# Second attention of a two-block kernel: a score bank for each head, query rotations by transfers and GpSimd, scores ahead of the last chunks, more selection rounds beside the queries

## The chip, the core and the metric

The kernel runs on one core of a Trainium2 chip, in one launch. The metric is the device time in microseconds (us); the engines are PE (TensorE), DVE (VectorE), ACT (ScalarE), POOL (GpSimd) and SP (the queue that issues transfers).

## What is computed

The reference chains a recurrent/attention block and a second block of two layers, all in fp32 on 512 positions with a model width of 1024. The change lies in the attention of the second block's first layer. Cut to that:

```
proj = h @ w_in                       # q: 16 heads of 64, k, v: 4 heads, an indexer: qi 8 heads, ki 1, wi 8
q = rope(rmsnorm(q)); k = rope(rmsnorm(k)); qi = rope(qi); ki = rope(layernorm(ki))
# rope: out = x * cos + swap_halves(x) * signed_sin, on all 64 rows of a head
for each block of 128 positions:
    score = sum over 8 heads of relu(qi . ki) * wi         # causal
    sel = the topk = 128 best keys of each position
    logits = q . k / 8, only the selected keys             # 16 heads
    o = softmax(logits) @ v
y = o @ w_out
```

After it come the residual, a gated feed-forward layer, a convolution layer and a second feed-forward layer; most of the time goes into their matrix products.

## The kernel before

**Tiles of weights.** All large products read one stream of weight tiles of 128 x 1024, `Tile(n)`, numbered from 0 to `T_END`. For each tile SP loads `RAW` (`raw`), ACT writes the rounded half `W_hi` (`split_hi`), DVE the rest `W_lo = RAW - W_hi` (`split_lo`, two instructions), and PE runs `linear`: for each of 8 chunks three products into one bank. PE waits on the semaphore `lo_done`, so a late `W_lo` stops it. Each engine has its own program, written out in order, and waits on semaphores.

**Tiles T_QKV2 to T_QKV2 + 16** make the indexer's inputs, keys, values, and last the eight query chunks (tiles T_QKV2 + 9 to + 16; "queries 6 to 13" in the rotation's count, two heads each). Between the products of these tiles PE also does the small work in `in_q(c)`: index scores for the last block of positions (the first four chunks), sums of squares (`query_columns`) and the rotation's product (`rot2`, a 128 x 128 permutation against the chunk, in bank 3).

**The query chunk's path.** ACT takes the bank out (`head_out`: a square, and `QN`); POOL multiplies `QN` by the cosine (`times_cosine`, into `QR`); PE turns `QN` (`rot2`); DVE multiplies the bank by the sine and adds (`turned`, `rope2_out`, into `Q`). POOL also sums the last block's index scores (`index_sum`, a multiply and an add for each head) and takes powers for the norms (`power`).

**Selection.** DVE finds the 128 best keys in 16 rounds of 8 for each of the three blocks n = 1, 2, 3 (`select`: a MAX8 and a MATCH_REPLACE8 over 256, 384 or 512 columns); after a block's last round two instructions write `BIAS`, which the scores add. Of the 48 rounds 7 stand ahead of query 6, 24 beside the queries (`ROUNDS_Q`), 17 inside the attention (`ROUNDS_S`).

**The attention** has 16 steps, s = 16 to 31, four groups of heads for each block of positions n; a step has 4 heads and n + 1 blocks of keys. Step s on the engines, each in its order:

- PE: `pv(s - 1)` (probabilities times values), `turn_probs(s)` (4 transposes for each block of keys), `spread(s)`, `qk(s + 2)`.
- ACT: `exps(s + 1)`, `spread_copy(s)`, `heads_hi(s - 2)`, `probs_out(s)` (one copy out of a bank for each block of keys).
- DVE: `sums_inverted(s)`, `y_scaled(s - 1)`, the step's rounds, `score(s + 2, h)` for 4 heads, `minus_max(s + 2)`.

`qk` writes its 4 heads to the banks `QK_BANKS` in turn, three of them, and each waits until the bank's last score is read:

```
dst = ps[QK_BANKS[m % 3]][:, 0:w]
pe.wait_ge(ttr_done, 64 + m - 2)
```

`turn_probs` has a bank for each block of keys (`PT_BANKS`, banks 0, 1, 4, 3). Here are the functions that the change touches, with their lines in the profile.

Of the kernel before, what the change touches and what calls it, by code (L numbers as in the profile page):

```python
# [207 lines left out]
def build(nc, x, stream, ada, crow, lru_w, prm, cst, rope1, pos, out):  # L208
    with ExitStack() as ctx:
# [34 lines left out]
        RL = at("RL", NRL * S, unit[6] + S * 8)  # L244
        WORK = at("WORK", S, unit[6] + S * 28)
# [33 lines left out]
        QN = at("QN", 3 * S, unit[4] + S * 12)  # L279
        RAB = at("RAB", 2 * S, unit[6])  # L280
# [52 lines left out]
        q_cos, sum_step = sem("q_cos"), sem("sum_step")  # L333
# [50 lines left out]
        def _(sp):  # L384
# [78 lines left out]
        def _(pe):  # L463
# [103 lines left out]
            def qk(s, heads=range(4)):  # L567
                g, n, keys = STEPS[s]
                w = len(keys) * P
                for h in heads:  # L570
# [35 lines left out]
            def spread(s):  # L606

                pe.wait_ge(recip_done, s - 15)
                if s > 16:
                    pe.wait_ge(yt_out, s - 16)  # L610
                for h in range(4):
                    odd, c = h % 2, (s % 2) * 24 + 16 + h
                    mm = pe.matmul(ps[6][odd * HD:(odd + 1) * HD, (2 + h // 2) * P:(3 + h // 2) * P],
                                   SM[:, c:c + 1].to_broadcast([P, HD]), cs("ident"), start=True, stop=True)
                mm.then_inc(spread_mm, 1)
# [98 lines left out]
            def rot2(i):  # L714
# [3 lines left out]
                pe.matmul(ps[3][:], cs("rot2"), ch(QN, (i + 1) % 3), start=True, stop=True).then_inc(rot_mm, 1)  # L718
# [114 lines left out]
            qk(17, (0, 1))  # L833
            rot2(13)
            query_columns(7)
            qk(17, (2, 3))
# [1487 lines left out]
```

## Time and profile before

| | before |
|---|---|
| median of 3 runs | 1755.95 us (1755.88 to 1760.2) |
| the profiled execution's own time | 1760.43 us |
| its span, first to last instruction | 1758.6 us |
| mean granted TensorE clock | 0.980 of full speed |
| PE busy | 1682.4 us, 96% |
| DVE busy | 1018.0 us, 58% |
| ACT busy | 703.0 us, 40% |
| POOL busy | 77.0 us, 4% |

Busy shares are means over the whole program. The stage that is changed lies between about 625 and 788 us of the span; what holds it is read from the stretches and instructions there.

### The profile page before, as it was taken

Reading aid. Unit: us, or ns where it says so; the run is one execution under the profiler, and the core shown is the slowest. Engines: PE = TensorE matmul, PEld = TensorE weight load, DVE = VectorE, ACT = ScalarE, POOL = GpSimd, SP = SyncE. Lnnn points to the kernel's source line nnn. Section 1 sums busy time; section 2 is a strip of 40 time slices with the busy share of each in tenths; the row PEclk is TensorE's granted clock in tenths of the full one; section 3 lists DMA queues with packets and bytes.
Section 4 is the critical chain, followed back from the end, with each engine's and each line's share of the span. In section 5 each row is a group of like instructions: output and inputs, shape, how many; then the busy total and the mean of one; then the engine's idle time right before and its main releaser. Section 6 shows DMA issues by size and latency. Waiting matters only on the chain.

```text
span 1758.6 us, 23023 instructions
## 1 busy us (share of the span) xinstructions
PE 1682.4 (96%) x7756; PEld 1338.5 (76%) x7756; DVE 1018.0 (58%) x2010; ACT 703.0 (40%) x1331; POOL 77.0 (4%) x62
## 2 busy tenths in 40 slices
PE   6998999999998998889999999999999899999999
PEld 5777677777887676547788888887888788888887
DVE  7788766666456688844655564467454533333344
ACT  5363666663344244763433322324223333332322
POOL 0020000000000064110000000000000000000000
PEclk9998999999998998999899999999999999999999
DMA  6453344444331121003355554353333233333333
GB/s 238 156 154 113 109 136 171 156 149 138 95 96 60 48 72 49 1 2 95 120 191 192 191 197 139 108 192 95 95 96 96 72 104 100 96 95 96 96 96 108
DMA packets 56775, 202.82 MB, mean 115 GB/s; under 512 B 6576, under 2 KB 6704, under 8 KB 56560
## 3 DMA queue, kind: packets, MB, share of 16 engines
q1 hardware_dynamic: 56688, 201.68, 35.2%
q8 instruction: 52, 0.85, 0.2%
q14 instruction: 35, 0.29, 0.0%
HBM read 198.38 MB, written 2.10 MB: 114 GB/s over the span
## 4 chain that ended last, share of the span: by engine, by line
PE 88%; DVE 8%; ACT 3%; issue 2%; DMA 0%; DVEq 0%; POOLq 0%; POOL 0%; ACTq 0%
PE bank L479 25%; PE bank L480 24%; PE bank L481 24%; PE bank L582 2%; PE bank L632 2%; PE bank L522 1%; PE bank L603 1%; PE bank L523 1%; DVE WORK L1934 1%; DVE SM L1933 1%; DVE W_lo L1418 1%; PE bank L525 1%; PE bank L528 1%; PE bank L502 1%; PE bank L504 1%
## 5 line engine op out<-in xcount | busy, mean ns | idle before, releaser
L479 PE MATMUL bank<-H_hi,W_hi 128*128 128x512 f32 x1336 | 534.7, 400 | 3.2 <-DVE W_lo L1418 2.0
L480 PE MATMUL bank<-H_lo,W_hi 128*128 128x512 f32 x1336 | 521.7, 391 | 0.0
L481 PE MATMUL bank<-H_hi,W_lo 128*128 128x512 f32 x1336 | 521.4, 390 | 0.0
L1418 DVE TENSOR_TENSOR W_lo<-RAW,W_hi 128x512 fp32r<-128x512 f32 x538 | 351.5, 692 | 199.1 <-ACT W_hi L907 185.3
L907 ACT ACTIVATE W_hi<-RAW 128x512 fp32r<-128x512 f32 x538 | 317.0, 625 | 281.0 <-PE bank L481 229.6
L479 PEld LDWEIGHTS bank<-H_hi,W_hi 128*128 128x128 f32 x1336 | 251.6, 188 | 74.8 <-issue 20.5
L480 PEld LDWEIGHTS bank<-H_lo,W_hi 128*128 128x128 f32 x1336 | 251.7, 188 | 54.3 <-issue 4.6
L481 PEld LDWEIGHTS bank<-H_hi,W_lo 128*128 128x128 f32 x1336 | 251.5, 188 | 53.6
L481 PE MATMUL bank<-A_hi,W_lo 128*128 128x512 f32 x352 | 137.0, 389 | 0.0
L480 PE MATMUL bank<-A_lo,W_hi 128*128 128x512 f32 x352 | 136.9, 389 | 0.0
L479 PE MATMUL bank<-A_hi,W_hi 128*128 128x512 f32 x352 | 136.9, 389 | 0.0
L1432 DVE CUSTOM_DVE_ANT_0 AW<-AW,CROW 128x1024 f32<-128x1024 f32 x96 | 118.1, 1231 | 9.7 <-DVE X L2118 3.7
L1145 ACT ACTIVATE G<-bank 128x512 f32<-128x512 f32 x60 | 35.9, 598 | 169.9 <-PE bank L481 169.9
L944 ACT CAST A_hi<-Y 128x512 f32 (+1 forms) x44 | 27.3, 620 | 184.9 <-DVE Y L2090 184.9
L2090 DVE TENSOR_TENSOR Y<-bank,G 128x512 f32<-128x512 f32 x44 | 30.4, 692 | 117.4 <-PE bank L481 117.2
L479 PEld LDWEIGHTS bank<-A_hi,W_hi 128*128 128x128 f32 x352 | 66.1, 188 | 13.8
L480 PEld LDWEIGHTS bank<-A_lo,W_hi 128*128 128x128 f32 x352 | 66.1, 188 | 13.7
L481 PEld LDWEIGHTS bank<-A_hi,W_lo 128*128 128x128 f32 x352 | 66.1, 188 | 13.7
L582 PE MATMUL bank<-KD,Q 64*128 64x256 f32 (+3 forms) x256 | 53.7, 447 | 16.8 <-DVE SM L2017 8.3
L2118 DVE SCALAR_TENSOR_TENSOR X<-bank,MOD,X 128x512 f32 x32 | 24.1, 752 | 76.0 <-PE bank L481 75.9
L2095 DVE TENSOR_TENSOR A_lo<-Y,A_hi 128x512 f32 (+1 forms) x44 | 30.5, 692 | 43.7 <-ACT A_hi L944 43.7
L582 PEld LDWEIGHTS bank<-KD,Q 64*128 64x128 f32 x256 | 26.9, 198 | 35.4 <-DVE SM L2017 16.9
(263 smaller groups left out, 2049.5 us busy)
## 6 DMA issues: line engine op xcount, KB each, us to landing
RAW<-weights SPq DMA_DIRECT2D x269, 512.0 KB, 3.7
AW<-ada SPq DMA_DIRECT2D x100, 512.0 KB, 3.7
X<-x_t SPq DMA_DIRECT2D x4, 512.0 KB, 6.5
y_t<-X SPq DMA_DIRECT2D x8, 256.0 KB, 2.0
LW<-lru_w SPq DMA_DIRECT2D x1, 1024.0 KB, 12.4
QX<-QR SPq DMA_DIRECT2D x40, 16.0 KB
CROW<-crow SPq DMA_DIRECT2D x1, 512.0 KB, 10.4
ROPE<-rope SPq DMA_DIRECT2D x1, 512.0 KB, 13.2
```

What stands on the lines that cost most here:

```text
L479: pe.matmul(dst, wh, ch(hi, k), start=(k == 0), stop=False)
L480: pe.matmul(dst, wh, ch(lo, k), start=False, stop=False)
L481: mm = pe.matmul(dst, wl, ch(hi, k), start=False, stop=(k == chunks - 1))
L582: mm = pe.matmul(dst, Q[rows, chunk * S + n * P:chunk * S + (n + 1) * P], KD[rows, k0:k0 + w], start=True, stop=True)
L632: mm = pe.matmul(ps[6][odd * HD:(odd + 1) * HD, 0:2 * P], V[:, at_col:at_col + HD], PT[:, c * S + odd * 2 * P:c * S + (odd + 1) * 2 * P], ...
L907: act.activation(W_hi[:, sl * HALF:(sl + 1) * HALF], RAW[:, c:c + HALF], fn).then_inc(hi_done, 1)
L944: act.copy(dst, ch(Y2, par)).then_inc(a_hi_done, 1)
L1145: act.activation(ch(G1, par), ps[PAIR_BANK if first else ga.bank][:], fn).then_inc(fn_done, 1)
L1418: dve.tensor_tensor(W_lo[:, w], RAW[:, c:c + HALF], W_hi[:, w], ALU.subtract).then_inc(lo_done, 1)
L1432: dve.tensor_tensor_reduce(out=w, in0=w, in1=CROW[:], scale=1.0, scalar=0.0, op0=ALU.mult, op1=ALU.add, accum_out=MODQ[:, q:q + 1]).then_i ...
L2090: dve.tensor_tensor(ch(Y2, par), ps[tile.bank][:], ch(G1, par), ALU.mult).then_inc(prod_done, 1)
L2095: dve.tensor_tensor(ch(A_lo[g % 2], jj), ch(Y2, par), ch(A_hi[g % 2], jj), ALU.subtract).then_inc(a_lo_done, 1)
```

## The change

- `QK_BANKS` gets a fourth bank, 3, one for each head of a step; `PT_BANKS` loses it, and `turn_probs` reuses its first bank for a fourth block of keys, behind the copy that empties it. `spread` moves from behind the transposes into them, ahead of the last (for n = 3 of the third) block of keys.
- The query chunks' rotation product on PE goes. SP copies the swapped halves of `QN` into a new `QX2` (`query_halves`, four transfers a chunk), POOL multiplies by the sine (`times_sine`), DVE only adds (`query_turned`), one chunk later than before.
- The multiplies of the last block's index scores go from POOL to ACT (`weighed`); POOL keeps the adds.
- The scores of step 16 come ahead of the last tile's split, those of steps 16 and 17 ahead of the last two query chunks' sums, which are added behind the scores of step 18.
- `ROUNDS_Q` goes from 24 rounds to 28, `ROUNDS_S` from 17 to 13.

```diff
+            def query_halves(i):
+                sp.wait_ge(head_in, i + 1)
+                if i >= 8:
+                    sp.wait_ge(rope_done, 10 + i - 1)
+                for head in (0, HD):
+                    for to, rows in ((head, head + HD // 2), (head + HD // 2, head)):
+                        sp.dma_start(QX2[to:to + HD // 2, (i % 2) * S:(i % 2 + 1) * S],
+                                     ch(QN, (i + 2) % 3)[rows:rows + HD // 2, :]).then_inc(q_half[i % 2], 16)
             for t in range(0, T_FFN0):
+                if T_QKV2 + 10 <= t <= T_QKV2 + 17:
+                    query_halves(t - T_QKV2 - 4)
...
-                        dst = ps[QK_BANKS[m % 3]][:, 0:w]
-                        pe.wait_ge(ttr_done, 64 + m - 2)
+                        dst = ps[QK_BANKS[h]][:, 0:w]
+                        if s > 16:
+                            pe.wait_ge(ttr_done, 64 + m - 3)
...
                 for c in range(len(keys)):
+                    if c == min(2, len(keys) - 1) and s >= 16:
+                        spread(s)
+                    if c == 3:
+                        pe.wait_ge(pt_out, PT_COUNT[s] + 1)
...
-                        mm = pe.transpose(ps[banks[c]][:, to:to + P], SB[:, src:src + P], cs("ident"))
+                        mm = pe.transpose(ps[banks[c % len(banks)]][:, to:to + P], SB[:, src:src + P], cs("ident"))
...
-                        if k == 3:
-                            rot2(6 + c - 1)
                     if c == 7 and k == 5:
...
+                        pe.wait_ge(rope_done, 10 + 10)
                         qk(16, (0, 1, 2))
...
             qk(16, (3,))
-            qk(17, (0, 1))
-            rot2(13)
             query_columns(7)
-            qk(17, (2, 3))
+            qk(17)
...
+            def weighed(u):
+                h = u - 12
+                rl, wcol = RL[:, (u % NRL) * S:(u % NRL + 1) * S], WI[:, 24 + h:25 + h]
+                act.wait_ge(relu_done, u + 1)
+                if h == 0:
+                    act.wait_ge(relu_used, u)
+                    act.mul(SCALL[:, 2 * S:3 * S], rl, wcol).then_inc(relu_used, 1)
+                    act.sem_inc(relu_scaled, 1)
+                else:
+                    act.mul(rl, rl, wcol).then_inc(relu_scaled, 1)
...
                     relu(13 + 2 * (c - 9))
+                    weighed(12 + 2 * (c - 9))
+                    weighed(13 + 2 * (c - 9))
                 head_out(c, c - 3, "q_g")
...
+            def times_sine(i):
+                pool.wait_ge(q_half[i % 2], 64 * ((i - 6) // 2 + 1))
+                pool.wait_ge(rope_done, max(10 + i - 1, 16))
+                if i == 13:
+                    pool.wait_ge(relu_used, IDX_UNITS)
+                pool.tensor_tensor(SIN13[:, :] if i == 13 else ch(RAB, 1 - i % 2), ch(QX2, i % 2), ROPE[:, S:2 * S], ALU.mult).then_inc(q_sin, 1)
...
             for i in range(6, 14):
-                if i in (11, 13):
-                    power(3 if i == 11 else 4)
-                if i >= 10:
-                    times_cosine(i)
+                if i == 11:
+                    power(3)
+                if i == 13:
+                    times_sine(12)
+                    power(4)
+                if 6 < i < 10:
+                    index_sum(2 * (i - 6))
+                times_cosine(i)
                 if i < 10:
-                    index_sum(2 * (i - 6))
-                    times_cosine(i)
                     index_sum(2 * (i - 6) + 1)
+                if 6 < i < 13:
+                    times_sine(i - 1)
+            times_sine(13)
...
+            def query_turned(i):
+                dve.wait_ge(q_cos, i - 5)
+                dve.wait_ge(q_sin, i - 5)
+                dve.tensor_tensor(ch(Q, i - 6), ch(QR, (i + 1) % 3),
+                                  SIN13[:, :] if i == 13 else ch(RAB, 1 - i % 2), ALU.add).then_inc(rope_done, 1)
...
             for c in range(10, 17):
-                split_lo(Tile(T_QKV2 + c + 1))
+                if c < 16:
+                    split_lo(Tile(T_QKV2 + c + 1))
...
-                rope2_out(6 + c - 10)
-                if c == 16:
+                if c > 10:
+                    query_turned(c - 5)
+                if c < 16:
+                    select(ROUNDS_Q[c - 10])
+                if c == 15:
                     query_roots(0)
...
-QK_BANKS = (2, 7, 5)
-PT_BANKS = ((4, 5), (0, 1, 4, 3))
+QK_BANKS = (2, 7, 5, 3)
+PT_BANKS = ((4, 5), (0, 1, 4))
...
-ROUNDS_Q = [4, 5, 4, 4, 4, 3]
-ROUNDS_S = [1, 1, 1, 1, 1, 2, 2, 2, 2, 2, 2]
+ROUNDS_Q = [6, 6, 4, 4, 4, 4]
+ROUNDS_S = [1, 1, 1, 1, 1, 1, 1, 1, 1, 2, 2]
```

On POOL, in the middle of the query chunks, the order before is this: a multiply and an add of index scores, a cosine (`QR`), a multiply and an add, and so on.

```order
L1365 TENSOR_SCALAR RL<-RL,WI 128x512
L1368 TENSOR_TENSOR SCALL<-SCALL,RL 128x512
L1376 TENSOR_TENSOR QR<-QN,ROPE 128x512
L1365 TENSOR_SCALAR RL<-RL,WI 128x512
L1368 TENSOR_TENSOR SCALL<-SCALL,RL 128x512
```

After the change the same place, from the cosine of query 6 to that of query 8 (`RAB<-QX` is the sine product of query 6):

```order
L1400 TENSOR_TENSOR QR<-QN,ROPE 128x512
L1392 TENSOR_TENSOR SCALL<-SCALL,RL 128x512 x2
L1400 TENSOR_TENSOR QR<-QN,ROPE 128x512
L1392 TENSOR_TENSOR SCALL<-SCALL,RL 128x512
L1407 TENSOR_TENSOR RAB<-QX_106,ROPE 128x512
L1392 TENSOR_TENSOR SCALL<-SCALL,RL 128x512
L1400 TENSOR_TENSOR QR<-QN,ROPE 128x512
```

The multiplies are gone, and the first sine product stands behind the cosine of query 7 and one add.

On DVE, from the last query chunk's split to the first score of step 16, before:

```order
L1418 TENSOR_TENSOR W_lo<-RAW,W_hi 128x512 x2
L1853 TENSOR_SCALAR VQ<-bank 128x24
L1868 TENSOR_TENSOR RAB<-bank,ROPE 128x512
L1873 TENSOR_TENSOR Q<-QR,RAB 128x512
L1836 TENSOR_TENSOR VQ<-VQ 128x32
L1837 SCALAR_TENSOR_TENSOR VQ<-VQ 128x32
L1838 SCALAR_TENSOR_TENSOR VQ<-VQ 128x32
L1860 TENSOR_SCALAR VQ<-VQ 128x32
L1861 TENSOR_SCALAR VQ<-VQ 128x32
L2017 ISA SB_68,SM<-bank,BIAS 128x128
```

and after the change (the last rounds, now of block 3, then the roots, one add and the score):

```order
L1976 MAX SM<-WORK 128x8
L1977 MATCH_REPLACE WORK<-SM,WORK 128x512
L1872 TENSOR_TENSOR VQ<-VQ 128x32
L1873 SCALAR_TENSOR_TENSOR VQ<-VQ 128x32
L1874 SCALAR_TENSOR_TENSOR VQ<-VQ 128x32
L1896 TENSOR_SCALAR VQ<-VQ 128x32
L1897 TENSOR_SCALAR VQ<-VQ 128x32
L1889 TENSOR_SCALAR VQ<-bank 128x24
L1915 TENSOR_TENSOR Q<-QR,RAB 128x512
L2061 ISA SB_68,SM<-bank,BIAS 128x128
```

The split of the next tile no longer stands here, nor the sine product; the split follows the first four scores.

On PE, a step with four blocks of keys (step 29), before: values product of step 28, 16 transposes, the spread, the scores' products of step 31, and the next values product.

```order
L632 MATMUL bank<-PT_69,V 64x256 x8
L603 MATMUL bank<-CS,SB_68 128x128 x16
L613 MATMUL bank<-CS,SM 64x128 x4
L582 MATMUL bank<-KD,Q 128x512 x4
L632 MATMUL bank<-PT_69,V 64x256 x8
```

and after the change:

```order
L652 MATMUL bank<-PT_69,V 64x256 x8
L634 MATMUL bank<-CS,SB_68 128x128 x8
L610 MATMUL bank<-CS,SM 64x128 x4
L634 MATMUL bank<-CS,SB_68 128x128 x8
L598 MATMUL bank<-KD,Q 128x512 x4
L652 MATMUL bank<-PT_69,V 64x256 x8
```

The spread stands between the transposes of the second and the third block of keys, and the last four transposes wait for `pt_out`, the first copy of this same step.

## Rows read from the trace of the kernel before

**Rows 1.** Page, part 1: busy us (share of the span) xinstructions.

```profile
PE 1682.4 (96%) x7756; PEld 1338.5 (76%) x7756; DVE 1018.0 (58%) x2010; ACT 703.0 (40%) x1331; POOL 77.0 (4%) x62
```

**Rows 2.** Stretches: length, busy PE, PEld, DVE, ACT, POOL, clock, DMA share, GB/s.

```profile
655.00:684.00 29.00, 29.00 (x139) 22.57 (x137) 27.00 (x60) 8.54 (x15) 16.91 (x10) 1.00 0.21 58
...
694.00:704.00 10.00, 9.66 (x48) 5.63 (x47) 6.51 (x30) 5.92 (x21) 0.39 (x1) 0.56 0.01 2
...
735.00:752.00 17.00, 14.31 (x88) 7.60 (x86) 15.02 (x44) 12.20 (x33) 2.19 (x3) 1.00 0.00 1
```

**Rows 3.** Waits from 640 to 684 us: in total, times, longest.

```profile
PEld bank L479 <- DVE W_lo L1418: 0.2, 1, 0.2
```

**Rows 4.** DVE in order of time, query chunks (start, us, instruction).

```profile
630.72 1.58 DVE L1418 TENSOR_TENSOR W_lo<-RAW,W_hi 128x512 fp32r<-128x512 f32 x2 [1.53 <-ACT W_hi L907]
...
659.32 0.68 DVE L1868 TENSOR_TENSOR RAB<-bank,ROPE 128x512 f32<-128x512 f32 x1
660.03 1.06 DVE L1873 TENSOR_TENSOR Q<-QR,RAB 128x512 f32<-128x512 f32 x1
661.24 0.56 DVE L1933 MAX8 SM<-WORK 128x8 f32<-128x384 f32 x1
...
666.24 1.29 DVE L1418 TENSOR_TENSOR W_lo<-RAW,W_hi 128x512 fp32r<-128x512 f32 x2
...
685.10 0.29 DVE L2017 CUSTOM_DVE_ANT_0 SB<-bank,BIAS 128x128 f32<-128x128 f32 x1
```

**Rows 5.** POOL and DVE in order of time, same stretch.

```profile
633.74 1.28 POOL L1368 TENSOR_TENSOR SCALL<-SCALL,RL 128x512 f32<-128x512 f32 x1
...
667.72 5.44 POOL L1354 TENSOR_TENSOR VQ<-VQ,HALF_NEG 128x32 f32<-128x32 f32 x1 [3.69 <-DVE VQ L1853]
...
633.84 1.73 DVE L1873 TENSOR_TENSOR Q<-QR,RAB 128x512 f32<-128x512 f32 x1
```

**Rows 6.** SP's swaps in the first attention; landing of the key copies.

```profile
99.18 2.65 SPq L421 DMA_DIRECT2D QX<-QR  x4
...
KD<-KD SPq DMA_DIRECT2D x4, 128.0 KB, 4.2
```

**Rows 7.** DVE in order of time, attention: y_scaled(17), (24), (25), (31); two scores.

```profile
700.93 0.39 DVE L1659 TENSOR_TENSOR YT<-bank,SPR 128x256 f32<-128x256 f32 x1
...
739.39 0.42 DVE L1659 TENSOR_TENSOR YT<-bank,SPR 128x256 f32<-128x256 f32 x1 [0.70 <-PE bank L632]
...
742.75 0.56 DVE L2017 CUSTOM_DVE_ANT_0 SB<-bank,BIAS 128x384 f32<-128x384 f32 x1
...
745.87 0.42 DVE L1659 TENSOR_TENSOR YT<-bank,SPR 128x256 f32<-128x256 f32 x1 [0.70 <-PE bank L632]
...
771.44 0.69 DVE L2017 CUSTOM_DVE_ANT_0 SB<-bank,BIAS 128x512 f32<-128x512 f32 x1 [3.11 <-PE bank L582]
...
787.07 0.42 DVE L1659 TENSOR_TENSOR YT<-bank,SPR 128x256 f32<-128x256 f32 x1 [5.43 <-PE bank L632]
```

**Rows 8.** PE in order of time: scores' products, then transposes.

```profile
747.70 1.98 PE L582 MATMUL bank<-KD,Q 64*128 64x512 f32 x6
751.18 1.12 PE L582 MATMUL bank<-KD,Q 64*128 64x512 f32 x2 [1.49 <-DVE SM L2017]
...
767.69 1.97 PE L603 MATMUL bank<-CS,SB 128*128 128x128 f32 x16
```

**Rows 9.** ACT in order of time: starts of exps(28), (29), (30), copies, exps(31).

```profile
753.27 0.81 ACT L1037 ACTIVATE SB<-SB,SM,VQ 128x512 f32<-128x512 f32 x1 [3.27 <-DVE SM L2026]
...
759.84 0.81 ACT L1037 ACTIVATE SB<-SB,SM,VQ 128x512 f32<-128x512 f32 x1 [1.27 <-DVE SM L2026]
...
766.85 0.81 ACT L1037 ACTIVATE SB<-SB,SM,VQ 128x512 f32<-128x512 f32 x1 [1.22 <-DVE SM L2026]
...
770.86 2.05 ACT L1051 COPY PT<-bank 128x512 f32<-128x512 f32 x4
...
774.29 0.81 ACT L1037 ACTIVATE SB<-SB,SM,VQ 128x512 f32<-128x512 f32 x1 [1.38 <-DVE SM L2026]
```

More of the change, by code:

```diff
@@ L244, in build @@
         RL = at("RL", NRL * S, unit[6] + S * 8)
+        SIN13 = at("SIN13", S, unit[6] + S * 16)
         WORK = at("WORK", S, unit[6] + S * 28)
@@ L279, in build @@
         QN = at("QN", 3 * S, unit[4] + S * 12)
+        QX2 = at("QX2", 2 * S, unit[4] + S * 24)
         RAB = at("RAB", 2 * S, unit[6])
@@ L585, in qk, with spread @@
                     mm.then_inc(qk_mm, 1)
+            def spread(s):
+                pe.wait_ge(recip_done, s - 15)
+                if s > 16:
+                    pe.wait_ge(yt_out, s - 16)
+                for h in range(4):
+                    odd, c = h % 2, (s % 2) * 24 + 16 + h
+                    mm = pe.matmul(ps[6][odd * HD:(odd + 1) * HD, (2 + h // 2) * P:(3 + h // 2) * P],
+                                   SM[:, c:c + 1].to_broadcast([P, HD]), cs("ident"), start=True, stop=True)
+                mm.then_inc(spread_mm, 1)
             def turn_probs(s):
@@ L602, in turn_probs @@
                         to = (h % 2 * 2 + h // 2) * P
-                        mm = pe.transpose(ps[banks[c]][:, to:to + P], SB[:, src:src + P], cs("ident"))
+                        mm = pe.transpose(ps[banks[c % len(banks)]][:, to:to + P], SB[:, src:src + P], cs("ident"))
                     mm.then_inc(pt_mm, 1)
[L606 to L615, printed above, removed]
             def pv(s):
@@ L717, in rot2 @@
                 pe.wait_ge(rope_done, 10 + i)
-                pe.matmul(ps[3][:], cs("rot2"), ch(QN, (i + 1) % 3), start=True, stop=True).then_inc(rot_mm, 1)
+                pe.matmul(ps[3][:], cs("rot2"), ch(QN, (i + 2) % 3), start=True, stop=True).then_inc(rot_mm, 1)
             def index(n, k):
@@ L840, in _ @@
             for s in range(16, 32):
+                if s > 16:
+                    pv(s - 1)
+                if s == 16:
+                    pe.wait_ge(head_var, 5)
+                turn_probs(s)
                 if s == 17:
@@ L843, in _ @@
                     pe.wait_ge(rope_done, 10 + 14)
-                if s > 16:
-                    pv(s - 1)
-                turn_probs(s)
-                if s == 16:
-                    pe.wait_ge(head_var, 5)
-                spread(s)
                 if s < 30:
@@ L1050, in probs_out @@
                     act.wait_ge(pt_mm, PT_COUNT[s] + c + 1)
-                    act.copy(ch(PT, c), ps[banks[c]][:]).then_inc(pt_out, 1)
+                    act.copy(ch(PT, c), ps[banks[c % len(banks)]][:]).then_inc(pt_out, 1)
             def y_region(t, s):
@@ L1209, in head_out @@
                 if gain is None:
-                    ins = act.copy(ch(QN, (i + 1) % 3), ps[tile.bank][:])
+                    ins = act.copy(ch(QN, (i + 2) % 3), ps[tile.bank][:])
                 else:
-                    ins = act.mul(ch(QN, (i + 1) % 3), ps[tile.bank][:], pr(gain))
+                    ins = act.mul(ch(QN, (i + 2) % 3), ps[tile.bank][:], pr(gain))
                 ins.then_inc(head_in, 1)
@@ L1931, in select @@
                     if q == 0 and n == 3:
-                        dve.wait_ge(sum_step, 8)
+                        dve.wait_ge(sum_step, 1)
                     link(dve.max(M8, score if q == 0 else work))
@@ L2016, in score @@
                 a = (s % 2) * 4 * S + h * w
-                dve.tensor_tensor_reduce(out=SB2[:, a:a + w], in0=ps[QK_BANKS[i % 3]][:, 0:w], in1=BIAS[:, n * S:n * S + w],
+                dve.tensor_tensor_reduce(out=SB2[:, a:a + w], in0=ps[QK_BANKS[h]][:, 0:w], in1=BIAS[:, n * S:n * S + w],
                                          scale=1.0, scalar=-3e38, op0=ALU.add, op1=ALU.max,
@@ L2028, in minus_max @@
                                   ALU.mult).then_inc(negm_done, 1)
+            dve.wait_ge(rope_done, 10 + 12)
             for h in range(4):
@@ L2032, in _ @@
             minus_max(16)
-            for h in range(2):
-                score(17, h)
-            rope2_out(13)
-            for h in range(2, 4):
+            split_lo(Tile(T_QKV2 + 17))
+            for h in range(4):
                 score(17, h)
             minus_max(17)
-            query_variance(2)
-            query_roots(1)
             for s in range(16, 32):
@@ L2047, in _ @@
                 if s < 30:
+                    if s + 2 == 18:
+                        query_variance(2)
+                        query_roots(1)
                     for h in range(4):
@@ L2052, in _ @@
                     minus_max(s + 2)
+                    if s + 2 == 18:
+                        query_turned(12)
+                        query_turned(13)
             y_scaled(31)
```

30 lines of the change are left out of this document (11 added, 19 removed).

## The prediction

> **What bounds the kernel now.** I read the page first: PE is busy for 96% of the span, DVE for 58% [rows 1]. A saving must therefore shorten PE's own sequence or a stretch in which PE waits. Next come the stretches. Beside the queries, 655 to 684 us, PE has no gap, but DVE has hardly one either: 27.0 of 29.0 us busy [rows 2]. The waits agree: PE waited 0.2 us for `W_lo` [rows 3]. The two engines are level there, and DVE decides when the attention begins, since its first score stands behind all its query work: from 630.72 to 685.10 us it runs almost without a pause [rows 4]. In the attention PE does wait: between 735 and 752 us it is busy for 14.3 of 17 us, and DVE for 15.0 [rows 2]. The place is the fourth head's score product: three heads go out at 747.70 us, the fourth stands 1.49 us at 751.18 until DVE has read a bank [rows 8], and the values product queues behind it. DVE's next `y_scaled` waits for that product. So a step is a loop through both engines: 6.48 us from `y_scaled(24)` to `y_scaled(25)` [rows 7].
>
> **The change, part by part.** All sums are differences to the profiled execution, whose own time was 1760.4 us against a span of 1758.6 and a median of 1755.95; the runs shown differ among themselves by 4.3 us, so I carry the difference over to the median.
>
> *Beside the queries* (DVE, until the first score at 685.10 us).
> - Added: one round of 384 columns at 1.25 us (four take 661.24 to 666.24, [rows 4]) and three of 512 at about 1.5 ((742.75 - 739.39 - 0.4) / 2, [rows 7]): 5.75. The two `BIAS` instructions of block 2 come along, about 1.0 at the pace of 0.68 for 512 columns.
> - Removed: seven sine products at 0.7 (659.32 to 660.03, [rows 4]): -5.0. The add of query 12 (-0.7) and a split (-1.3, [rows 4]) go behind the scores.
> - ACT's two multiplies, about 0.5 each like its copies [rows 9], stand ahead of `QN` and `W_hi`; DVE already waits for `W_hi` at 630.72 us [rows 4], so it starts 1.0 later. ACT itself has time.
> - Two new waits of DVE for POOL. The sine of query 6 stands behind the cosine of query 7 and an add: 3 x 1.28 us [rows 5] behind `QN`, while DVE is there about 2.2 behind it (half a `W_hi`, a split): 1.6. At query 10 POOL has 5.44 for the power and 2 x 1.28 behind it [rows 5], 8.0, where DVE comes after an add, four rounds and a split, 7.1: 0.9. Queued behind each wait are DVE's rounds and the next tile's `W_lo`.
> - Collisions. A DVE add took 1.73 us beside a POOL instruction [rows 5], where the usual pass is 0.68; others took 1.06 and, for a split, 1.58 instead of 1.29 [rows 4]. Over the seven chunks I put them at 4 us. POOL keeps 23 instructions of 512 columns (eight multiplies go, eight sine products come) but loses the longer kind, and DVE has fewer with two SBUF inputs: I take -2, with -4 and +4 as ends.
>
> Sum: 5.75 + 1.0 - 5.0 - 0.7 - 1.3 + 1.0 + 1.6 + 0.9 - 2 = +1.25. The first score comes at about 686.3. PE loses seven rotation products there, but DVE decides, so that is worth nothing; it only ends its last tile some 2 to 3 us earlier and then idles.
>
> *SP.* Four transfers a chunk hold its queue for about 2.65 us [rows 6]; the weight loads behind them go out four tiles ahead, so nothing waits. Only the last chunk counts: its swap waits for the add of query 11 (about 686), takes 2.0 to the fourth issue and 4.2 to land [rows 6], then a sine (1.3) and an add (0.7): 694.3 before PE may form the scores of step 19. Then `y_scaled(16)`, a round, scores and roots follow on DVE, 5 us, and PE runs at low clock somewhere here as before (mean 0.56 in 694 to 704 us, [rows 2]), 2 to 3 us more. I take `y_scaled(17)` at 702.1 against 700.93 [rows 7]: +1.2.
>
> *Steps 18 to 25.* Before, `y_scaled(17)` to `y_scaled(25)` is 44.9 us [rows 7]. Four rounds leave (steps 21 to 24): -6.0. With four banks the fourth head's product no longer waits for a score of its own step; the loop through DVE and PE opens, and a step costs the fullest engine. For 6.48 us of step the stretch 735 to 752 gives 5.7 DVE (4.2 without one round), 5.5 PE (its modelled ends overlap) and 4.7 ACT [rows 2]; so steps of 384 columns go to 5.1. That leaves 1.2 over the eight steps beyond the rounds: -7.2. The ends are -6 (only the rounds) and -9.
>
> *Steps 26 to 31.* From `y_scaled(25)` to the exponentials of step 28 DVE holds it alone, two rounds, `BIAS` and four scores, as before: 0. The next start of exponentials (6.57 later, 753.27 to 759.84, [rows 9]) can follow ACT: 4 x 0.8, 0.6 and three copies of 0.5, with a wait 5.4: -1.1. Then the new wait bites. The fourth block's transposes of step 28 need ACT's first copy of this step, which stands behind ACT's exponentials of step 29: 3.2 + 0.55 + 0.5 = 4.25 us after their start. Behind it on PE: a quarter of 1.97 for the transposes [rows 8], a first pair of heads 1.0, four scores of 0.65 (each 0.69 less overlap, [rows 7]), the maximum and three hand-overs 0.4: 8.7 us until the next exponentials, against 7.01 and 7.44 [rows 9]: +1.7 and +1.3. Without the wait it would be 6.6. In the last step the spread, and so ACT's copies, start 0.5 to 1 earlier: -0.4. Sum +1.5. What follows 787.07 us [rows 7] is unchanged.
>
> Total: 1.2 - 7.2 + 1.5 = **-4.5 us**, 1751.5 us.
>
> **The rivals.**
> - *Forecast (0.45)*: the terms above, -2 to -7.
> - *The gain comes whole (0.27)*. The waits for POOL are hidden (DVE still has rounds to do when the sine is ready) and the copy wait costs less, because ACT's first copy finds the exponentials done: -2.5 - 3 on top, -10 us, 1746. For it: POOL was idle a good part of 655 to 684 us (16.9 of 29 busy, [rows 2]). Against: order of POOL and of ACT is fixed.
> - *No gain (0.17)*: DVE beside the queries is 4 us later than I have it, PE idles longer before the first scores, so the low clock lasts longer, and the rounds' gain goes there: 1755 to 1757. That would be the change not doing what it says: the rounds are moved to a place that is just as full.
> - *Slower (0.11)*: POOL holds DVE off its operands. If every one of the 12 halves of splits and 6 adds lost 1.05 as the one in rows 5 did, 19 us stand against the 2 in my sum; +12, 1768. It decides from about 10 us, when some ten of the 18 wait out a POOL instruction; with about half of the time covered by POOL and half an instruction the mean wait, I get 6.
>
> The Trainium skill (GPSIMD Engine Reference, Specifications) says that GpSimd shares its SBUF interfaces with VectorE and contends with Vector instructions with two SBUF inputs. The 1.73 us row agrees with it. The rule speaks against moving the sine from a product with a PSUM input on DVE to one in SBUF on POOL; taken to the full it is the slower rival, and with it the sum would be +12 instead of -4.5.
>
> **How the numbers follow.** The likeliest case gives 1751.5; alone its range is 1749 to 1754. The 8-in-10 range takes in most of the whole gain and of no gain: 1745 to 1759, its upper end also for the 4.3 us between runs. No change to be told from noise is within 0.3%, 5.3 us. Faster than that: a third of the forecast and nearly all of the whole gain, 0.41. Slower: 0.11. The rest, 0.48, lies within.
>
> **What the profile after would show.** Right: the first score at 685 to 688 us; DVE idle before the adds of queries 6 and 10 with POOL as releaser; no wait of the score products for DVE in steps 18 to 27; some 5.1 us a step in 22 to 24; a wait of PE for ACT's copy in the transposes of steps 28 and 29, and 8.7 us between the exponentials of 29, 30 and 31. Wrong: DVE short of work beside the queries, `W_lo` late at PE by more than 1 us a tile, transposes of step 28 without a wait, or a low clock that lasts into step 20.

## The result, and the profile after

The changed kernel takes 1762.92 us (median of 7 runs, 1762.2 to 1767.32) against 1755.95 (7 runs, 1755.54 to 1760.2): ratio 1.0038, 95% interval 1.0029 to 1.0048. The forecast was 1751.5 us; it came out 7.0 us slower instead of 4.5 faster, outside the range.

The profiled execution of after took 1763.02 us, span 1761.2. Part 1 of its page:

```profile
PE 1671.9 (95%) x7740; PEld 1332.3 (76%) x7740; DVE 1017.3 (58%) x2002; ACT 707.8 (40%) x1339; POOL 75.7 (4%) x62
```

PE is busy for 10.5 us less than in [rows 1], and yet the kernel is longer: what was added is waiting. The stretches of after that answer to [rows 2] (length; busy PE, PEld, DVE, ACT, POOL; clock, DMA share, GB/s), and one more, in the last steps:

```profile
655.00:684.00 29.00, 26.00 (x126) 20.85 (x124) 26.58 (x59) 9.45 (x15) 15.70 (x8) 0.96 0.45 123
694.00:704.00 10.00, 7.47 (x40) 5.00 (x42) 6.09 (x26) 5.70 (x21) 0.73 (x1) 0.50 0.01 2
735.00:752.00 17.00, 14.91 (x112) 8.54 (x110) 13.86 (x42) 12.80 (x33) 1.85 (x2) 1.00 0.00 1
755.00:785.00 30.00, 24.33 (x152) 13.49 (x152) 7.62 (x25) 17.04 (x42) 2.19 (x3) 0.83 0.00 1
```

The first row shows PE short of work beside the queries (26.0 of 29 us), where it had no gap before. The last shows nobody busy: PE 24.3 of 30 us, DVE 7.6, ACT 17.0, and a clock of 0.83. The same stretch of before:

```profile
755.00:785.00 30.00, 27.16 (x192) 15.79 (x192) 10.47 (x35) 22.62 (x55) 3.56 (x5) 1.00 0.00 1
```

So the last steps are the first place to look. What PE waits for in the attention of after (us in total, times, longest):

```profile
PE bank L610 <- DVE YT L1695: 6.4, 5, 2.1
PE bank L634 <- ACT PT L1067: 6.4, 4, 1.9
PE bank L652 <- ACT PT L1067: 4.1, 7, 0.8
PE bank L598 <- DVE SM L2061: 3.6, 1, 3.6
PE bank L610 <- DVE SM L1683: 1.8, 1, 1.8
```

The wait that the fourth bank was to remove is gone: before, the row for it read

```profile
PE bank L582 <- DVE SM L2017: 8.3, 11, 1.5
```

In its place stand two new ones: the spread (L610) for `y_scaled` of the step before, and the fourth block's transposes (L634) for ACT's first copy. The first costs little: 5.8 of its 6.4 us are still there in e7 (below), which keeps every gain up to step 27.

**Reading the stage in pieces.** Single executions of either kernel lie up to 5 us apart, and the mean clock of a run goes with it (of the kernel before, 1755.0 us at 0.983 and 1760.6 at 0.979); in the traces the start of query 6 alone moves by up to 5 us (624.5 to 629.5 us). So I measure from a mark at the start of the stage, ACT's `QN` of query 6 (629.10 us before, 625.32 after), to the first score, and on by `y_scaled` of steps 17, 25, 27 and 31. These pieces repeat within some 0.1 us wherever the code in them is alike. The rows of after that answer to the last of [rows 4] and to [rows 7]:

```profile
685.23 0.29 DVE L2061 CUSTOM_DVE_ANT_0 SB<-bank,BIAS 128x128 f32<-128x128 f32 x1
...
700.37 0.39 DVE L1695 TENSOR_TENSOR YT<-bank,SPR 128x256 f32<-128x256 f32 x1
...
741.22 0.42 DVE L1695 TENSOR_TENSOR YT<-bank,SPR 128x256 f32<-128x256 f32 x1
...
789.20 0.42 DVE L1695 TENSOR_TENSOR YT<-bank,SPR 128x256 f32<-128x256 f32 x1 [5.07 <-PE bank L652]
```

The table has every kernel of this study (us; the last column is the median with the ratio to the kernel before on the same chip):

```
                          query 6 to    to      to      to      to    sum    median, ratio
                          first score  y(17)   y(25)   y(27)   y(31)
before                        56.0     15.8    44.9    14.6    26.6  158.0   1755.95
after                         59.9     15.1    40.9    13.9    34.1  163.9   1762.92  1.0038
e1  banks undone              59.9     17.1    41.5    16.2    26.6  161.3   1762.12  1.0022
e2  before + banks            56.0     15.1    40.8    14.9    34.5  161.4   1762.06  1.0019
e3  rounds undone             53.6     16.2    43.9    13.9    33.2  160.8   1759.01  1.0012
e4  before + rounds           64.0     17.7    41.0    14.6    26.6  163.9   1759.81  1.0011
e5  fill, last steps          59.9     15.1    40.9    13.9    30.5  160.3   1760.71  1.0015
e6  fill, first scores        59.9     15.4    40.8    13.9    34.1  164.0   1764.18  1.0037
e7  fourth bank late          59.9     15.1    40.0    13.9    26.6  155.5   1755.26  0.9991
e8  e7, rounds undone         53.6     16.1    44.0    13.9    27.0  154.5   1752.27  0.9967
e9  GpSimd narrow             51.5     14.3    42.3    13.9    32.2  154.2   1753.99  0.9985
e10 wide fill, first scores   59.9     15.1    40.9    13.9    34.2  163.9   1765.14  1.0046
e11 e8, filled                53.6     21.3    44.9    13.9    26.9  160.5   1759.62  1.0018
e12 e8, one round forward     57.1     15.1    41.9    13.8    27.0  154.9   1756.50  0.9988
e13 before, GpSimd narrow     56.9     15.6    44.4    14.6    26.6  158.1   1757.63  1.0003
e14 sine on the vector        62.1     16.1    39.8    14.7    34.4  167.1   1766.37  1.0045
e15 e8, sine on the vector    52.8     16.2    42.3    13.9    26.6  151.7   1753.63  0.9972
```

The differences of the sums agree with the ratios within 2.5 us; only for e4 they don't (+6.0 in the pieces, +1.9 by the ratio, interval +0.4 to +3.5). In its trace what follows step 31 is 2.3 us shorter than before (969.3 against 971.5 us), in code that is the same; why stays open. I trust the pieces for where time went and the ratio for how much.

### The profile page after: what moved, and what is told of

Read it like the earlier page. It is cut to its first block, busy times and chain, and to the rows that moved or that the text cites. A ratio compares the mean times of both kernels' runs of the same rounds, so it can differ in the third digit from the quotient of the medians.

```text
span 1761.2 us, 23024 instructions
## 1 busy us (share of the span) xinstructions
PE 1671.9 (95%) x7740; PEld 1332.3 (76%) x7740; DVE 1017.3 (58%) x2002; ACT 707.8 (40%) x1339; POOL 75.7 (4%) x62
## 4 chain that ended last, share of the span: by engine, by line
PE 83%; DVE 7%; ACT 5%; issue 3%; POOL 1%; DMA 0%; DVEq 0%; POOLq 0%; ACTq 0%
PE bank L494 24%; PE bank L496 24%; PE bank L495 24%; PE bank L598 1%; PE bank L537 1%; PE bank L538 1%; DVE SB L2061 1%; PE bank L652 1%; PE bank L634 1%; DVE W_lo L1454 1%; ACT SB L1053 1%; PE bank L540 1%; PE bank L543 1%; PE bank L517 1%; POOL SCALL L1392 1%
## 5 line engine op out<-in xcount | busy, mean ns | idle before, releaser
L1454 DVE TENSOR_TENSOR W_lo<-RAW,W_hi 128x512 fp32r<-128x512 f32 x538 | 356.3, 701 | 201.1 <-ACT W_hi L923 186.2
L598 PE MATMUL bank<-KD,Q 64*128 64x256 f32 (+3 forms) x256 | 44.6, 468 | 12.8 <-DVE SM L1655 9.2
L2142 DVE TENSOR_TENSOR A_lo<-Y,A_hi 128x512 f32 (+1 forms) x44 | 30.5, 692 | 42.6 <-ACT A_hi L960 42.6
L494 PE MATMUL bank<-YA_hi,W_hi 128*128 128x512 f32 x128 | 50.1, 392 | 3.7 <-POOL YA_lo L1436 2.0
```

The lines of the kernel that those rows point to most:

```text
L494: pe.matmul(dst, wh, ch(hi, k), start=(k == 0), stop=False)
L598: mm = pe.matmul(dst, Q[rows, chunk * S + n * P:chunk * S + (n + 1) * P], KD[rows, k0:k0 + w], start=True, stop=True)
L1454: dve.tensor_tensor(W_lo[:, w], RAW[:, c:c + HALF], W_hi[:, w], ALU.subtract).then_inc(lo_done, 1)
L2142: dve.tensor_tensor(ch(A_lo[g % 2], jj), ch(Y2, par), ch(A_hi[g % 2], jj), ALU.subtract).then_inc(a_lo_done, 1)
```

## The experiments

**Undoing and doing one part at a time (e1 to e4).** e1, from after:

```diff
-QK_BANKS = (2, 7, 5, 3)
-PT_BANKS = ((4, 5), (0, 1, 4))
+QK_BANKS = (2, 7, 5)
+PT_BANKS = ((4, 5), (0, 1, 4, 3))
-                    if c == min(2, len(keys) - 1) and s >= 16:
-                        spread(s)
-                    if c == 3:
-                        pe.wait_ge(pt_out, PT_COUNT[s] + 1)
```

(with the spread behind `turn_probs` and the scores' banks and waits of before; `turn_probs` waits for nothing inside a step again).

> The changed kernel with its bank part undone: scores again in three banks by turns, the probabilities' fourth block in a bank of its own, the row sums spread behind the transposes. Theory A (the three probability banks are the loss: y_scaled of step 27 to step 31 took 34.1 us after, 26.6 before): that stretch falls back to 26.6 to 28 us, steps 18 to 25 give back 1 to 3 us of what the fourth score bank won, and the time is 1757 to 1759 us. Theory B (the loss is made in the query stage, by vector work and GpSimd holding each other up, and by the low clock behind it): the last four steps stay over 32 us or the time stays at 1761 to 1763 us.

Last piece 26.6 us; steps up to 27 gave back 5.0 (74.9 from the first score against 69.9); 1762.12 us. Theory A's piece is exact, its total is missed: 1762.12 is the time that theory B named. The fourth score bank had won more than I thought, and taken as a whole the bank part makes up only some 2.6 us of the loss (163.9 against 161.3).

e2 puts the same four edits into before, from step 18 on.

> The kernel before with the bank part alone (four score banks and three for the probabilities from step 18 on, the spread inside the transposes). Theory A: y_scaled of step 27 to step 31 goes from 26.6 to 32 to 34 us, the steps before it win 0 to 2, and the time is 1760 to 1763 us. Theory B: 1755 to 1757 us, since the query stage is untouched.

34.5 us in the last steps, 4.5 won ahead of them (theory A had 32 to 34 and 0 to 2), 1762.06. Banks alone lose 3.4 us: theory A, with both of its sizes too small.

e3 and e4 exchange the two tables:

```diff
-ROUNDS_Q = [6, 6, 4, 4, 4, 4]
-ROUNDS_S = [1, 1, 1, 1, 1, 1, 1, 1, 1, 2, 2]
+ROUNDS_Q = [4, 5, 4, 4, 4, 3]
+ROUNDS_S = [1, 1, 1, 1, 1, 2, 2, 2, 2, 2, 2]
```

> The changed kernel with the table of rounds of before (24 beside the queries, 17 beside the attention steps). Theory A (the moved rounds pay: +5.75 us in front, -6.0 behind, and the open loop on top needs them): 1762 to 1766 us. Theory B (rounds in front cost in full, and with them PE waits for W_lo and the clock falls, while behind the scores they were half hidden): 1757 to 1760 us, first score some 4 to 6 us earlier.

> The kernel before with the table of rounds of after alone. Theory A: front +5.75 us, steps 20 to 24 -6.0 us, so 1755 to 1757 us. Theory B (in front in full, behind only in part): 1758 to 1761 us. By the terms of the prediction 1755.7 us.

e3: first score 6.3 us earlier, 3.2 given back by step 31, 1759.01. e4: first score 8.0 later, 2.0 won back, 1759.81. Both times lie within theory B: four rounds and `BIAS` cost their full 6 to 8 us in front and return 2.0 and 3.2 behind. Its other half, `W_lo` late at PE, shows too: PE waits 2.2 us for it in after, 0.9 in e3.

The piece from `y_scaled(17)` to `y_scaled(25)`, cut at step 20, tells what the two parts do there (us):

```
         y(17) to y(20)   y(20) to y(25)
before        13.5             31.4
e2 banks      13.4             27.4
e4 rounds     13.6             27.5
e3            16.5             27.4
after         14.9             26.0
```

From step 20 on, the banks alone win 4.0 us and the rounds alone 3.9, but both together 5.4: each takes away the same waiting, so their gains do not add up. With four banks in place, the four rounds are worth 1.4 us. The 16.5 us of e3 go with a low clock over steps 18 and 19 (mean 0.50 and 0.65), which in after ends in step 18.

**The last steps (e5, e7).** PE in order of time in step 28 of after: transposes of block 3, of block 4 (behind 1.90 us of waiting), scores, values; and block 4 of step 29:

```profile
756.51 0.66 PE L634 MATMUL bank<-CS,SB 128*128 128x128 f32 x4
759.06 0.66 PE L634 MATMUL bank<-CS,SB 128*128 128x128 f32 x4 [1.90 <-ACT PT L1067]
759.65 3.67 PE L598 MATMUL bank<-KD,Q 64*128 64x512 f32 x8
763.25 1.95 PE L652 MATMUL bank<-PT,V 128*64 128x256 f32 x16
...
769.28 0.66 PE L634 MATMUL bank<-CS,SB 128*128 128x128 f32 x4 [1.89 <-ACT PT L1067]
```

and ACT beside it, which answers to [rows 9]; exponentials of steps 29, 30, 31 and the copies:

```profile
754.67 0.82 ACT L1053 ACTIVATE SB<-SB,SM,VQ 128x512 f32<-128x512 f32 x1 [0.41 <-DVE SM L2070]
...
758.43 2.02 ACT L1067 COPY PT<-bank 128x512 f32<-128x512 f32 x4
...
764.89 0.81 ACT L1053 ACTIVATE SB<-SB,SM,VQ 128x512 f32<-128x512 f32 x1 [4.43 <-DVE SM L2070]
...
775.08 0.81 ACT L1053 ACTIVATE SB<-SB,SM,VQ 128x512 f32<-128x512 f32 x1 [4.41 <-DVE SM L2070]
```

The loop is closed and can be read off: exponentials, first copy, last transposes, scores, maximum, exponentials. It takes 10.2 us. Shortly ahead of the step's scores (x8) PE stood idle, and they took 3.67 us. e5 puts work there:

```diff
-                        mm = pe.transpose(...)
+                        for _ in range(4 if s >= 28 and c == 2 else 1):
+                            mm = pe.transpose(...)
```

> The changed kernel, but in steps 28 to 31 TensorE repeats the transposes of the third block three times more (the same values into the same bank), in front of the wait for ACT's first copy, so that the 1.9 us of idle time there hold work. Theory C (the wait itself makes 8.7 us a step, as forecast, and the rest of the 10.2 us is the low clock that follows the idle time, 3.4 us of it in each of these steps): no low clock between 755 and 785, 8.6 to 9.0 us a step, y_scaled of step 27 to step 31 in 30 to 31.5 us instead of 34.1, and 1759 to 1761 us in all. Theory D (the clock has nothing to do with that idle time, or the step is 10.2 us by its waits alone): 34 us or more, 1763 us or more.

PE of e5, the same place (L635 are its transposes), and the stretch of 30 us that begins 4 us later as its stage does:

```profile
760.41 1.97 PE L635 MATMUL bank<-CS,SB 128*128 128x128 f32 x16
762.98 0.66 PE L635 MATMUL bank<-CS,SB 128*128 128x128 f32 x4 [0.60 <-ACT PT L1068]
763.56 1.99 PE L598 MATMUL bank<-KD,Q 64*128 64x512 f32 x8
```

```profile
759.00:789.00 30.00, 27.28 (x224) 19.11 (x222) 7.29 (x25) 19.99 (x49) 3.38 (x5) 1.00 0.01 1
```

The clock is 1.00 and the scores take 1.99 us. The step is 9.0 us, the last piece 30.5 instead of 34.1. Theory C: of the 7.5 us lost there, 3.6 are the low clock (1.2 of 2.4 GHz) behind the idle time and 3.9 the wait itself, with whatever the spread's new place costs (no run has one without the other).

e7 avoids the wait instead: four score banks up to step 29, and from step 28 on bank 3 for the fourth block and the spread behind the transposes again.

```diff
-                        dst = ps[QK_BANKS[h]][:, 0:w]
+                        dst = ps[SCORE_BANK(s, h)][:, 0:w]
-                            pe.wait_ge(ttr_done, 64 + m - 3)
+                            pe.wait_ge(ttr_done, 64 + m - (2 if m > 58 else 3))
...
-PT_BANKS = ((4, 5), (0, 1, 4))
+PT_BANKS = ((4, 5), (0, 1, 4, 3))
...
+def SCORE_BANK(s, h):
+    return QK_BANKS[h if s < 30 else (4 * (s - 30) + h) % 3]
```

> The changed kernel, but from step 28 on the fourth block of the probabilities has its own bank 3 again and the spread stands behind the transposes, and the scores of steps 30 and 31 go by turns through three banks, as before the change. Theory A (the loss of the last steps is the wait for ACT's first copy and the low clock behind it, and the opened loop pays up to step 27): y_scaled of step 27 to 31 in 26.5 to 28 us, the steps up to 27 as in the changed kernel (69.9 us from the first score), 1755.5 to 1758 us. Theory B (the fourth score bank gains only what the last steps lose anyway): over 1760 us.

> The same with the table of rounds of before. By the sum over the stretches measured so far (53.6 us from query 6 to the first score, 73.9 from there to step 27, 26.6 to step 31: 154.1 against 158.0 of the kernel before): 1753 to 1755.5 us, faster than before. If the low clock at the first steps lasts longer when rounds leave the front (27 us of it in the run with the rounds put back), up to 1757 us.

e7: 26.6 in the last piece, 69.0 up to step 27, 1755.26 us, level with before. e8, with the rounds of before as well, has its first score 6.3 us earlier and gives 5.3 back: 1752.27, ratio 0.9967 (0.9954 to 0.998), faster than both kernels and a little below the range expected. e12 moves one round to the front again:

> The version with the late fourth bank and the rounds of before, but one round more beside the queries (of 384 columns, 1.25 us, and through it one round that was of 384 becomes of 512), and one less in step 21. If a round in front costs its length and one behind saves it where two stand in a step: 1751 to 1752.5 us. If rounds behind are half hidden (7 us in front bought 4 behind in the pair of runs measured): 1752.5 to 1753.5 us.

First score 3.5 us later, 3.1 returned: nothing gained, and 1756.50 us lies above both of the ranges that I had named. One round of about 1.3 us put the first score off by far more than its length; PE waits 3.2 us for `W_lo` there.

**The clock at the first steps (e6, e10, e11).** After shows half clock from 684.7 to 705.2 us, e8 from 679.2 to 706.5. e6 and e10 fill PE's 3.6 us of waiting, behind `query_columns(7)` (moved ahead for it) and ahead of the last score of step 16 and those of step 17; e6 with 14 products of 128 columns on 64 rows, e10 with

```diff
+            for n in range(15):
+                pe.matmul(ps[QK_BANKS[3]][:], H_hi[:, 0:P], ch(H_hi, 0), start=True, stop=True)
```

> The changed kernel, but TensorE fills the 3.6 us in which it waits for the first scores by the vector engine with 14 repeats of the last score matmul of step 16 (same values, same bank), behind the column sums of query 13. Theory C (the 20.5 us of low clock at 685 to 705 follow from that idle time): the low clock starts later or lasts 3 to 10 us, the stretch from the first score to y_scaled of step 20 takes 27.5 to 29 us instead of 30.0, and the time is 1760.5 to 1762 us. Theory D (it comes from the many short waits of the first steps, whatever stands before): the low clock begins within 7 us of the first scores all the same, and the time is 1762.5 to 1764 us.

> As the run with 14 narrow repeats in front of the first scores, but the fill is 15 matmuls of 128x128 by 512 columns on the normed input (into the free score bank). Theory C (the clock follows what TensorE does in that gap, and narrow matmuls of 128 columns were too little): the low clock begins after 690 or lasts under 14 us, first score to y_scaled of step 20 in 26.5 to 28.5 us. Theory D (the clock falls for what comes behind the first scores, whatever fills the gap): 20 us of low clock from 684 to 688 on and 30 us as before.

The stretches of after, of e6 and of e10 (two):

```profile
684.70:705.20 20.50, 14.47 (x78) 9.36 (x80) 15.81 (x71) 11.02 (x39) 9.29 (x5) 0.50 0.15 39
```

```profile
683.90:704.40 20.50, 15.50 (x86) 10.63 (x84) 15.54 (x68) 11.02 (x39) 9.31 (x5) 0.50 0.14 39
```

```profile
684.00:697.00 13.00, 7.48 (x51) 5.49 (x50) 12.38 (x53) 6.46 (x24) 8.59 (x5) 1.00 0.25 72
697.20:707.40 10.20, 8.71 (x46) 5.54 (x48) 5.88 (x28) 4.66 (x16) 0.73 (x1) 0.51 0.01 2
```

The narrow products left the clock as it was, the wide ones held it 10 us longer; they differ in rows and in columns, and no run tells which counts. And the time didn't move: first score to `y_scaled(20)` is 30.0 us in after and in e10. In the first 10 us DVE, with 12.4 of 13 us busy, decides, and PE's clock costs nothing: theory C has the clock of e10 right and its time wrong. The low clock only came later, and in both kernels it covers step 18. There it does cost: from `y_scaled(17)` to `y_scaled(18)` are 5.73 us at a mean clock of 0.58 in after, 5.07 at 0.66 in e7, where these steps have the same code, and 4.25 at 1.00 in e2. e11 fills e8 there and, with 4 wide products a step, in steps 16 to 19.

> The version with the late fourth bank and the rounds of before (1752.3 us), plus the 15 wide fills in front of the first scores and 4 matmuls of 128x128 by 512 columns into the free bank 1 ahead of the spread in each of steps 16 to 19. Theory C (the 27 us of low clock cost it 3 to 5 us in steps 16 to 21, and work in the gaps holds the clock): low clock under 10 us there, first score to y_scaled of step 20 in 28 to 30 us instead of 32.7, 1748 to 1750.5 us. Theory D: the low clock stays and the fills come on top, 1752 to 1757 us.

Its clock:

```profile
682.00:712.00 30.00, 27.18 (x144) 13.72 (x143) 19.36 (x82) 14.87 (x50) 6.69 (x6) 1.00 0.07 18
```

The clock is full as theory C has it, but my fills were too long: the first, 5.3 us where 1.6 were idle, put off the first step by 5 us. 1759.62, above both ranges; what a full clock is worth over the first steps as a whole stays open.

**The query stage (e9, e13, e14, e15).** DVE of after beside POOL (start, us, instruction):

```profile
634.50 0.43 DVE L1976 MAX8 SM<-WORK 128x8 f32<-128x256 f32 x1
...
635.49 3.04 DVE L1454 TENSOR_TENSOR W_lo<-RAW,W_hi 128x512 fp32r<-128x512 f32 x2
...
671.28 2.38 DVE L1454 TENSOR_TENSOR W_lo<-RAW,W_hi 128x512 fp32r<-128x512 f32 x2
674.91 1.69 DVE L1915 TENSOR_TENSOR Q<-QR,RAB 128x512 f32<-128x512 f32 x1 [1.25 <-POOL RAB L1407]
```

```profile
633.78 1.27 POOL L1400 TENSOR_TENSOR QR<-QN,ROPE 128x512 f32<-128x512 f32 x1 [0.38 <-ACT QN L1228]
635.01 1.29 POOL L1392 TENSOR_TENSOR SCALL<-SCALL,RL 128x512 f32<-128x512 f32 x1
636.26 1.71 POOL L1407 TENSOR_TENSOR RAB<-QX,ROPE 128x512 f32<-128x512 f32 x1
```

A pair of splits took 3.04 us beside the last two of three POOL instructions in a row, 1.29 alone [rows 4], while the MAX8 beside the first took its usual 0.43. e9 leaves work out: POOL multiplies 32 columns instead of 512 for queries 6 to 12, and DVE adds `QN` to itself.

> The changed kernel with part of the work left out: for the queries 6 to 12 GpSimd multiplies 32 of the 512 columns by cosine and by sine (same number of instructions, same waits), and the vector engine adds the unturned query to itself, so the result is another. Theory E (GpSimd's long products and the vector engine hold each other up: the pairs of W_lo took 2.4 to 3.0 us instead of 1.3, two adds 1.7 instead of 0.7, and one add waited 1.25 for a sine product): from QN of query 6 to the first score 51 to 54 us instead of 59.9, no low clock at 650 to 657, and 1755 to 1758 us. Theory F (the vector engine's own rounds fill the stretch, the collisions lie in its slack): 57 us or more, 1760 us or more.

e13 does the same with the cosine product of before (POOL's index multiplies and adds stay).

> The kernel before with part of the work left out: for the queries 6 to 12 GpSimd multiplies 32 of the 512 columns by cosine, and the vector engine adds the unturned query instead of the product. In the changed kernel the same cut shortened query 6 to first score from 59.9 to 51.5 us. Theory G (the collisions are as large before, so the change added none): 56.0 falls by 6 us or more, to 50 or less. Theory H (the change made them, with seven sine products more on GpSimd): 56.0 falls by 1 to 4 us, to 52 to 55, and 1752 to 1756 us in all.

From `QN` of query 6 to the first score in before, after, e9, e13:

```profile
629.10:685.10 56.00, 54.97 (x254) 40.80 (x252) 50.07 (x110) 20.07 (x36) 40.23 (x25) 1.00 0.26 77
```

```profile
625.32:685.23 59.91, 53.50 (x248) 41.27 (x246) 54.76 (x114) 24.87 (x43) 36.28 (x24) 0.94 0.37 102
```

```profile
625.06:676.60 51.54, 50.22 (x247) 38.71 (x246) 47.44 (x113) 24.81 (x43) 20.38 (x24) 1.00 0.43 118
```

```profile
626.40:683.31 56.91, 55.23 (x254) 40.72 (x252) 49.01 (x111) 20.57 (x37) 31.98 (x25) 1.00 0.26 77
```

In after GpSimd's long products cost 8.4 us of this stretch (theory E; the whole, 1753.99 us, is below the 1755 to 1758 that I had named). DVE's busy time falls by 7.3 us without them (54.76 to 47.44), and the wait of 1.25 for the sine at query 10 is gone. So is PE's one long wait for a split:

```profile
PE bank L494 <- DVE W_lo L1454: 2.2, 1, 2.2
```

Behind it PE ran at half clock from 650.6 to 657.4 us in after, and not in e9. Before, the same cut brought nothing, 0.9 us more: the time of neither G nor H. It had little to take away, as DVE's busy time fell by 1.1 us only (50.07 to 49.01). And PE set the pace there, busy for 54.97 of 56.0 us without a wait; with the cut `QN` of queries 6 to 9 still comes every 8.54 us. So the collisions of after were mostly made by the change, as theory H has it, if not by the products that it names (e14). The splits show it, before and after (between the bars: us in all, mean ns of one):

```profile
L1418 DVE TENSOR_TENSOR W_lo<-RAW,W_hi 128x512 fp32r<-128x512 f32 x16 | 11.4, 755 | 2.0 <-ACT W_hi L907 1.5 <-DVE KD L1900 0.2
L1454 DVE TENSOR_TENSOR W_lo<-RAW,W_hi 128x512 fp32r<-128x512 f32 x12 | 13.6, 1172 | 2.3 <-ACT W_hi L923 2.1
```

An estimate of all collisions of the stretch, from the durations of splits, adds and `BIAS` less those that the same instructions have alone (1.29 a pair of splits, 0.68 an add, 0.72 and 0.92 for the two of `BIAS` at 256 and 384 columns): 4.0 us before, 9.6 after, 2.2 in e9, 2.9 in e13. The Trainium skill (GPSIMD Engine Reference, Specifications) has GpSimd contend with Vector instructions that have two SBUF inputs or run in a two-port mode; the splits (two inputs in SBUF) and the MAX8 (one) above agree with it. `BIAS` has a TENSOR_SCALAR of 256 columns with one SBUF input that took 1.27 us in after and 0.29 in e13; whether it ran in a two-port mode no row tells.

e14 and e15 put the sine product back on DVE, from the swapped halves in SBUF, in after and in e8:

```diff
+                link(dve.tensor_tensor(sine, ch(QX2, i % 2), ROPE[:, S:2 * S], ALU.mult))
-                dve.wait_ge(q_sin, i - 5)
```

> The changed kernel with all products by sine back on the vector engine (0.7 us each, from the transferred halves; TensorE still turns nothing). Theory H (what GpSimd's sine products take from the vector engine by collisions and waits is about what they save it): +4.9 us of products and -3 to -6 of collisions and the 1.25 us wait, so 58 to 61 us from query 6 to the first score instead of 59.9. Theory I (the products are saved nearly in full and the collisions come from the cosine products alone): 63 to 65 us, 1766 us or more in all.

> The same in the version with the late fourth bank and the rounds of before (53.6 us from query 6 to the first score, 1752.3 us). Theory H: 52.5 to 55 us and 1751 to 1754 us. Theory I: 57 us or more and 1755 to 1757 us.

e14: 62.1 us, 2.2 more, between the two theories' numbers, with theory I's time (1766.37): of the 4.9 us of products GpSimd had saved less than half. The splits stay as long as in after (mean 1144 ns against 1172; e9, with narrow cosines too, has 783). So it is not the sine products that hold the splits up. The two runs point to the cosines, and which part of the change brought them beside the splits is not separated. e15: 52.8 us, 0.8 less than e8: there GpSimd saved nothing (theory H). Its time, 1753.63 us and 0.9972 (0.9959 to 0.9985), can't be told from e8's; both beat the kernel before and the changed one.

## Why the prediction was wrong, point by point

- **Steps 26 to 31: +1.5 forecast, +6.8 measured, the largest error.** The mechanism was named in full: the fourth block's transposes wait for ACT's first copy. The size was not. The 8.7 us a step are 9.0 at full clock (e5), and the term for the clock was missing: 10.2 us with it. At full clock these steps would have come to +3.2 (e5); the other 3.6 are the clock. I looked for low clock only where [rows 2] showed it, at the start; but a new wait of 1.9 us in each step brings its own. -1.1 for the first of these steps was about right (6.57 to 5.7 us); the -0.4 at the end was not there: step 31 lost 1.3, and 0.1 at full clock (e5).
- **Steps 18 to 25: -7.2 forecast, -4.1 measured.** The step that failed is the sum of the two gains: four rounds at their full length, -6.0, and 1.2 more for the open loop. From step 20 on the rounds alone win 3.9 us, the banks alone 4.0, both 5.4, since both remove the same waiting. The steps with 384 columns came to 5.0, 5.3, 5.5 and 5.6 us, not 5.1. And steps 18 to 20, where the forecast had a gain, took 1.4 us more than before (14.9 against 13.5), with the low clock over step 18. Against e1 the fourth bank also wins 2.0 us up to step 17 and 2.3 in steps 26 and 27, where I had put nothing for it.
- **The first score: +1.25 forecast, +3.9 measured.** Rounds and `BIAS`, 6.75 forecast, were 6.3 to 8.0 (e3, e4). The steps that failed are "DVE decides, so that is worth nothing" and the -2 for collisions. Before, PE decided: [rows 2] had it busy for 29.00 of 29.00 us, DVE for 27.00. So the rotation products taken off it counted: `QN` of queries 6 to 9 come every 7.68 us instead of 8.54. The collisions of before were sized about right (4 forecast, 4.0 by the estimate above), but the change brought them to 9.6 instead of 2. Four of six pairs of splits now take 2.4 to 3.0 us, beside POOL's cosines and adds, and four more rounds had made DVE the bound, so that all of it counted. Without waits and collisions my sum was +0.75, and e9, which leaves most of them out, shows -4.5; for waits and collisions I had +0.5, and they are 8.4. The two errors, -5.2 and +7.9, partly cancelled, and that is luck. So is it that 685.23 us lies in the forecast's 685 to 688: query 6 itself began 3.8 us earlier in this trace.
- **SP and `y_scaled(17)`: +1.2 forecast, +3.2 measured**; the late first score is all of it. The add of query 13 came 8.8 us behind the first score (694.04), where 8.0 had been worked out, and the half clock up to `y_scaled(16)` costs nothing (e10).
- **The waits for POOL**: 0.9 forecast at query 10, 1.25 measured. The one at query 6 did not show; DVE was kept by its splits instead.
- **The rivals.** "No gain" and "slower" had the right places, the first scores and GpSimd's hold on DVE, and 0.28 between them; a loss clear of noise had 0.11. But the greatest loss, in the last steps, stood only as a small term of the forecast. The terms give +5.9 us in all between query 6 and step 31 against -4.5 forecast; the median's +7.0 leaves 1.1 that I can't place.

## What to carry to other kernels

A buffer taken from one place to open a loop closes another: write down the new loop, from the wait round to itself, at full length, and price it also at half clock if PE idles in it each time. Before costing work on two engines that look level, cut the work of each alone: what lies in slack costs nothing until the edit makes that engine the bound, and then all of it is due at once. Two edits that remove the same waiting are worth little more than one of them (4.0 and 3.9 us alone, 5.4 together): don't add their gains. Sharing a scarce bank by stage (e7: four for scores early, four for probabilities late) kept both gains.

## What the runs showed of the hardware

- 1.9 us of waiting ahead of score products, once a step, came with half clock over those products (3.67 us in after, 3.56 in e2, instead of 1.99); with repeated transposes in the gap it did not (e5).
- At the first scores, 14 products of 64 rows and 128 columns (3.90 us) did not put off the half clock; 15 of 128 rows and 512 columns (3.65 us) put it off by 10 us (e6, e10).
- One step of the attention, step 18, took 4.25 us at a mean clock of 1.00 (e2), 5.07 at 0.66 (e7), 5.73 at 0.58 (after).
- Beside GpSimd's instructions of 512 columns a pair of DVE's splits took up to 3.04 us instead of 1.29 and an add up to 1.76 instead of 0.68; the rounds never lengthened (of 48 MAX8 none over 0.70 us, of 48 MATCH_REPLACE8 none over 0.68).
